# S5 by chunks of four state tiles, with two sums on GpSimd, and routing three rows earlier

## The chip, the cores and the metric

One core of one Trainium2 chip runs the whole kernel as one program. The time is device microseconds of one execution; less is better. TensorE is called PE here, VectorE DVE, ScalarE ACT, GpSimd POOL and SyncE SP.

## What is computed

A decoder trunk of two layers over 256 tokens of width 1024, all in float32. Layer 0 is attention and a gated unit behind one input product; layer 1 is an S5 state-space layer with a sigmoid GLU. Behind each comes a PEER expert layer, and a norm at the end. The change touches S5, its GLU, the norms and the routing of PEER. Cut to these:

```python
def s5_block(h, ...):                       # 64 groups of 16 channels, 64 complex states each
    xr = einsum('bsgc,gpc->bsgp', u, bbr)   # input product, real; xi alike
    # complex diagonal recurrence over the tokens, per state:
    _, _, sr, si = associative_scan(combine, (a_r, a_i, xr, xi), axis=1)
    y = einsum('bsgp,gcp->bsgc', sr, c_re) - einsum('bsgp,gcp->bsgc', si, c_im)
    g = gelu(y + d_skip * h)
    return g * sigmoid(g @ glu_w + glu_b)

def peer(h, wq, subkeys, u_tab, v_tab):
    q = (h @ wq).reshape(t, 8, 2, 128)      # 8 heads, two halves
    sc = einsum('thpc,pkc->thpk', q, subkeys)
    # top 16 of 128 in each half, top 16 of their 256 sums: idx, gate = softmax
    act = gelu(einsum('td,tkd->tk', h, u_tab[idx]))
    return einsum('tk,tkd->td', gate * act, v_tab[idx])
```

## The kernel before, in words

**Rows of experts.** PEER is most of the work. For each of 2 layers, 2 token tiles of 128 tokens and 8 heads there is a group of 16 chosen experts per token: 32 groups, 512 rows. One row is one gather of the u and v rows of 128 experts (one per token), 128 x 2048 floats or 1 MB, issued by POOL (L434) into one of nine ring buffers; a dot product on DVE of the u half with `h` (`dot_product`, L1264); three small instructions on ACT that make gelu times gate and a diagonal matrix of it (`weights`, L620, L623, L626); and two products on PE of the diagonal with the v half (`expert`, L869), which add up in PSUM. POOL issues the gather of row g when the expert products of row g-9 are done. Row r of a phase of 128 rows is called row r below.

**Everything else hangs between the rows.** `between()` writes out by hand which stage runs in which row; every engine walks through the same list and takes the functions that it has. So on each engine the order is fixed: the stages of a row, then on DVE the routing step of that row (`ROUTE`: steps in rows 3, 5, 7, 9 and 11 of each group of 16, for the group that follows), then the row's own dot product. On PE the expert products of row g-1 follow the stages of row g. Layer 1's S5 runs inside phases 1 and 2 (the 128 rows from 128, and from 256), one token tile in each: while DVE and PE do the experts of one token tile of layer 0 they also do S5 of the other.

**S5.** The states are 32 tiles of 128. Before the scan they are turned by the angle of each token, so that the recurrence is a real one, and turned back behind it. The work goes by pairs of state tiles, one pair every five rows from row 9, 16 pairs: PE makes the input product (`s5_in`, L813, 8 matmul records in the trace), DVE turns it (`s5_rot`: L1137 and L1138, products with cosine and sine over 512 elements, then the two sums L1140 and L1141 over 256), two rows later DVE scans (`s5_scan`: L1150, four scans of 128 elements, L1153 and L1154 turn back, L1157 keeps the last state in the first token tile, and every second pair L1104 makes the angles' fraction), and PE makes the output product (`s5_out`, L832, 16 records, into PSUM with tokens as partitions). Two buffers hold the products of the turn. ACT makes the cosine and sine tables for a chunk of four state tiles.

**Behind S5** come `s5_sum` (L1166, L1171: the skip term), `s5_gelu` on ACT, `gate_T` and `gT_copy` (transposes), two GLU products with bias and tanh (`glu_mm` in `stream` L676, `glu_bias` L1182, `glu_sum`), the next norm, and from row 107 four queries, one every five rows (`query`: q_mm in three pieces through L676, transposes, scores). The weights of these products are 2 MB blocks that SP loads into two buffers, each when the product two blocks earlier is done. SP also loads eleven times a vector broadcast to 128 partitions (`load_vec`), two buffers.

**Norms.** `norm_h` (L909) writes x times rstd times gain to `h` for every norm, and PE transposes it.

## Time and profile before

| | |
|---|---|
| median of 3 runs | 1623.54 us (1619.47 to 1626.23) |
| profiled execution | 1625.63 us |
| its span, first to last instruction | 1623.9 us |
| mean granted clock of PE | 0.941 of full |
| read from HBM | 605.19 MB |
| moved by gathers | 536.90 MB |

The profiled execution is 1.7 us longer than its span, which lies outside the instructions. Busy time says how long an engine had work, the lists of waits say what an idle engine waited for, and the stretches say where the DMA queues ran below their best rate.

### The profile page before, as it was taken

Reading aid. Unit: us, or ns where it says so; the run is one execution under the profiler, and the core shown is the slowest. Engines: PE = TensorE matmul, PEld = TensorE weight load, DVE = VectorE, ACT = ScalarE, POOL = GpSimd, SP = SyncE. Lnnn points to the kernel's source line nnn. Section 1 sums busy time; section 2 is a strip of 40 time slices with the busy share of each in tenths; the row PEclk is TensorE's granted clock in tenths of the full one; section 3 lists DMA queues with packets and bytes.
Section 4 is the critical chain, followed back from the end, with each engine's and each line's share of the span. In section 5 each row is a group of like instructions: output and inputs, shape, how many; then the busy total and the mean of one; then the engine's idle time right before and its main releaser. Section 6 shows DMA issues by size and latency. Waiting matters only on the chain. (4 is left out here: it accounts for less than half of the span.)

```text
span 1623.9 us, 15247 instructions
## 1 busy us (share of the span) xinstructions
PE 1372.6 (85%) x3816; PEld 629.7 (39%) x3816; DVE 1140.5 (70%) x2821; ACT 760.9 (47%) x2074; POOL 597.2 (37%) x517
## 2 busy tenths in 40 slices
PE   7999889887697888898999788887898988887776
PEld 3544334433342444454444344444434432222222
DVE  2347865666666898998654898988865486666664
ACT  2325542454344656655443655656433354444443
POOL 0025333343243443334332443433334254444441
PEclk9999899999799898789999998999799999999999
DMA  9569999999799998799999999989899899999996
GB/s 358 185 245 408 409 390 414 383 375 417 302 416 417 418 361 327 313 386 376 405 414 379 416 391 356 342 323 382 326 394 413 315 414 421 422 421 422 422 422 256
DMA packets 106406, 607.22 MB, mean 374 GB/s; under 512 B 9296, under 2 KB 9424, under 8 KB 40784
## 3 DMA queue, kind: packets, MB, share of 16 engines
q0 software_dynamic: 73728, 536.90, 81.9%
q1 hardware_dynamic: 32592, 69.37, 11.5%
q8 instruction: 30, 0.49, 0.1%
q14 instruction: 56, 0.46, 0.1%
HBM read 605.19 MB, written 1.05 MB: 373 GB/s over the span
## 5 line engine op out<-in xcount | busy, mean ns | idle before, releaser
L869 PE MATMUL ps<-rings,dgs 128*128 128x512 f32 x1824 | 902.3, 635 | 179.1 <-ACT dgs L626 178.6
L434 POOL DMA_INDIRECT rings<-in_uv_tab_dram,idx x456 | 530.9, 1164 | 854.0 <-PE ps L869 671.7
L1264 DVE CUSTOM_DVE_ANT_0 rings<-rings,h 128x1024 f32<-128x1024 f32 x456 | 547.5, 1223 | 127.0 <-DMA rings<-in_uv_tab_dram,idx 112.3
L869 PEld LDWEIGHTS ps<-rings,dgs 128*128 128x128 f32 x1824 | 346.7, 200 | 667.2 <-issue 345.7
L620 ACT ACTIVATE gel<-dots 128x1 f32<-128x1 f32 x512 | 103.1, 201 | 548.2 <-DVE dots L1264 537.6
L626 ACT ACTIVATE dgs<-cst,wgt 128x128 f32<-128x128 f32 x512 | 206.2, 403 | 37.0 <-issue 2.5
L676 PE MATMUL ps<-wst,hT 128*128 128x512 f32 x384 | 180.0, 607 | 10.4 <-DMA wst<-in_wq_dram 8.1
L623 ACT ACTIVATE wgt<-gel,share 128x1 f32<-128x1 f32 x512 | 151.5, 296 | 37.5 <-issue 2.8
L869 PE MATMUL ps<-dgs 128*128 128x512 f32 x224 | 113.5, 631 | 17.6 <-ACT dgs L626 17.6
L676 PEld LDWEIGHTS ps<-wst,hT 128*128 128x128 f32 x384 | 73.9, 195 | 103.3 <-issue 101.7
L434 POOL DMA_INDIRECT dgs<-in_uv_tab_dram,idx x56 | 65.0, 1161 | 104.2 <-PE ps L869 95.0
L1041 DVE COPY mem<-ps 128x512 f32<-128x512 f32 x16 | 11.1, 692 | 119.2 <-PE ps L668 119.2
L1264 DVE CUSTOM_DVE_ANT_0 dgs<-dgs,h 128x1024 f32<-128x1024 f32 x56 | 68.5, 1223 | 17.2 <-DMA dgs<-in_uv_tab_dram,idx 15.0
L869 PEld LDWEIGHTS ps<-dgs 128*128 128x128 f32 x224 | 42.4, 199 | 78.8 <-issue 41.3
L620 ACT ACT_TABLE_LOAD x56 | 71.8, 1283 | 1.8
L832 PE MATMUL ps<-mem 128*128 128x32 f32 x512 | 67.7, 288 | 0.0
L832 PEld LDWEIGHTS ps<-mem 128*128 128x128 f32 x512 | 65.1, 205 | 6.6 <-issue 3.5
L676 PE MATMUL ps<-rings,hT 128*128 128x512 f32 x128 | 58.8, 611 | 2.0 <-DVE scr L936 1.2
L510 ACT ACTIVATE mem<-ps 128x512 f32<-128x512 f32 x16 | 9.6, 597 | 88.2 <-PE ps L676 88.2
L1264 DVE DVE_READ_ACCUMULATOR2_ANT dots<- 128x1 f32 x512 | 42.3, 83 | 0.0
L607 ACT ACT_TABLE_LOAD x32 | 41.1, 1283 | 0.8
L1137 DVE TENSOR_TENSOR mem<-ps,mem 128x512 f32<-128x512 f32 x32 | 22.0, 689 | 21.2 <-issue 10.7
(177 smaller groups left out, 973.5 us busy)
## 6 DMA issues: line engine op xcount, KB each, us to landing
wst<-in_wq_dram SPq DMA_DIRECT2D x15, 2048.0 KB
wst<-in_w_out_dram SPq DMA_DIRECT2D x4, 2048.0 KB
wst<-in_glu_w_dram SPq DMA_DIRECT2D x4, 2048.0 KB
rings<-in_uv_tab_dram,idx POOLq DMA_INDIRECT x456
rings<-in_w_in_dram SPq DMA_DIRECT2D x3, 2048.0 KB, 16.6
vec<-in_vecs_dram SPq DMA_DIRECT2D x11, 512.0 KB
rings<-in_w_in_dram SPq DMA_DIRECT2D x2, 1024.0 KB, 8.7
dgs<-in_w_in_dram SPq DMA_DIRECT2D x1, 2048.0 KB, 19.4
```

The lines of the kernel that those rows point to most:

```text
L434: nc.gpsimd.indirect_dma_start(out=ring[g % RING], out_offset=None, in_=uv_tab, in_offset=bass.IndirectOffsetOnAxis(ap=idx[n % 4][:, s:s + ...
L510: A.activation(qs, ps[:, 2, :], ACT.Copy).then_inc(qs_act, 1)
L607: A.activation(gexp[n % 2][:, :], cs[n % 2][:, :], ACT.Exp, bias=ncs[n % 2][:, :], accum_out=gsum[n % 2][:, :]).then_inc(exp_ok, 1)
L620: A.activation(gel[i][:, every], dots[i][:, every], ACT.Gelu_apprx_tanh)
L623: A.activation(wgt[i][:, c], gel[i][:, c], ACT.Copy, scale=share[i][:, c])
L626: A.activation(diag[:, (g + k) % DIAGS, :], ident, ACT.Copy, scale=wgt[i][:, c]).then_inc(diag_ok, 1)
L676: ins = PE.matmul(ps[:, bank, :], lhs[:, k, :], rhs[:, k, :], start=(k == 0), stop=(k == KC - 1))
L832: ins = PE.matmul(o, d, m[:, j, v, :], start=(q == 0), stop=(q == 3))
L869: ins = PE.matmul(ps[:, 4 + 2 * t + b, :], diag[:, g % DIAGS, :], ring[g % RING][:, D + b * BANK:D + (b + 1) * BANK], start=(g % (PH * TOP ...
L1041: V.tensor_copy(qT, four(3)).then_inc(qt_dve, 1)
L1137: V.tensor_tensor(by_cos, x4, cos, ALU.mult)
L1264: V.tensor_tensor_reduce(out=u, in0=u, in1=h[:, t, :], scale=1.0, scalar=0.0, op0=ALU.mult, op1=ALU.add, accum_out=dots[n % 2][:, s:s + 1] ...
```

## The change

What it does, by parts:

- **S5 by chunks.** A chunk of four state tiles every ten rows takes the place of two pairs. Turn and back-turn are two instructions each over 1024 elements, the scans two over 512: the four tiles' scans of 128 tokens lie end to end, and the decay tensor (`s5_decay`, written by ACT) is zero at each first token, which starts a new scan. The state that is carried to the second token tile is added to its first element. There is one buffer for each product of the turn in place of two.
- **The two sums on POOL** (`s5_add`): 512 elements each, all operands in SBUF. POOL does the stages of row r ahead of the gather of row r+7. DVE's scan waits for them (`add_ok`).
- **The input product ahead.** `s5_in` of a chunk stands seven rows ahead of its slot, into the other half of each PSUM bank.
- **Output product turned round.** `s5_out` has the 32-column C matrices as weights and the states as moving data, so that y comes out with channels as partitions; the skip term is one more matmul with a diagonal of `d_skip`. So gelu writes straight into `hT`; `s5_sum`, `gT_copy` and the copy of the transpose fall away, and `gate_T` only makes the g that `glu_sum` multiplies by. The GLU bias is a one-row matmul.
- **Norms.** The mixing norms no longer write `h`: PE multiplies x by a diagonal of rstd, the gain goes in at the copy; the first two norms transpose x itself, and rstd is put in behind the input product. Vectors are loaded three times in place of eleven, plus one small table and two rows of 4 KB.
- **Slots.** Routing steps stand in rows 0, 2, 4, 6 and 8 of a group. GLU begins at row 89, the norm at row 97, and the queries at row 103, one every six rows. `q_copy` and `q_score` come one row later in a query and `q_keep` two. `route_index` does both halves in one instruction each.

The core of the diff, first the order of the work:

```diff
 GROUPS = 2 * T * PH
 RING = 9
+AHEAD = 7
 PACE = 1
...
-ROUTE = {3: "route_keys", 5: "route_pairs", 7: "route_best", 9: "route_index", 11: "route_gate"}
-EXP_AT = 9
+ROUTE = {0: "route_keys", 2: "route_pairs", 4: "route_best", 6: "route_index", 8: "route_gate"}
+EXP_AT = 6
...
-PRELUDE = [("norm_sq", 0), ("norm_ms", 0), ("norm_sd", 0), ("norm_h", 0), ("norm_T", 0), ("hT_copy", 0),
+PRELUDE = [("norm_T", 0), ("hT_copy", 0), ("norm_sq", 0), ("norm_ms", 0), ("norm_sd", 0), ("norm_r", 0),
...
-        at(n, slot + 5, ("q_copy", phase, b))
-        at(n, slot + 6, ("q_score", phase, b))
-        at(n, slot + 7, ("q_keep", phase, b))
+        at(n, slot + 6, ("q_copy", phase, b))
+        at(n, slot + 7, ("q_score", phase, b))
+        at(n, slot + 9, ("q_keep", phase, b))
...
+    def mix_norm(n, slot, m):
+        for i, name in enumerate(("norm_sq", "norm_ms", "norm_sd", "norm_r", "norm_d", "norm_T", "hT_copy")):
+            at(n, slot + i, (name, m))
...
-        norm(g, 3, 4 + 2 * t)
-        for pair in range(S5_TILES // 2):
-            slot = 9 + 5 * pair
-            at(g, slot, ("s5_mm", t, pair))
-            at(g, slot + 1, ("s5_rot", t, pair))
-            at(g, slot + 2, ("s5_turns", t, pair))
-            at(g, slot + 3, ("s5_scan", t, pair))
-            at(g, slot + 4, ("s5_tables", t, pair))
-        at(g, 89, ("s5_last", t))
-        at(g, 90, ("s5_sum", t))
-        at(g, 91, ("s5_gelu", t))
-        at(g, 92, ("gate_T", t))
-        at(g, 93, ("gT_copy", t))
+        mix_norm(g, 3, 4 + 2 * t)
+        at(g, 3, ("s5_turns", t, 0))
+        at(g, 4, ("s5_frac", t, 0))
+        at(g, 6, ("s5_tables", t, 0))
+        for c in range(KC):
+            slot = 11 + 10 * c
+            at(g, slot - 1 if c == 0 else slot - 7, ("s5_in", t, c))
+            at(g, slot, ("s5_decay", t, c))
+            at(g, slot + 1, ("s5_rot", t, c))
+            at(g, slot + 2, ("s5_add", t, c))
+            at(g, slot + 3, ("s5_scan", t, c))
+            at(g, slot + 4, ("s5_cmat", t, c))
+            at(g, slot + 5, ("s5_back", t, c))
+            if c + 1 < KC:
+                at(g, slot + 3, ("s5_turns", t, c + 1))
+                at(g, slot + 4, ("s5_frac", t, c + 1))
+                at(g, slot + 6, ("s5_tables", t, c + 1))
+            at(g, slot + 6, ("s5_out", t, c))
+            if c % 4 == 3:
+                at(g, slot + 8, ("s5_gelu", t, c // 4))
...
-            at(g, 94 + 2 * b, ("glu_mm", t, b, 0, 4))
-            at(g, 95 + 2 * b, ("glu_mm", t, b, 4, 8))
-            at(g, 96 + 2 * b, ("glu_bias", t, b))
-            at(g, 97 + 2 * b, ("glu_sig", t, b))
-            at(g, 98 + 2 * b, ("glu_sum", t, b))
-        norm(g, 101, 5 + 2 * t)
+            at(g, 89 + 2 * b, ("glu_mm", t, b, 0, 4))
+            at(g, 90 + 2 * b, ("glu_mm", t, b, 4, 8), ("gate_T", t, b))
+            at(g, 93 + 2 * b, ("glu_sig", t, b))
+            at(g, 94 + 2 * b, ("glu_sum", t, b))
+        norm(g, 97, 5 + 2 * t)
         for b in range(4):
-            query(g, 107 + 5 * b, 2 + t, b)
+            query(g, 103 + 6 * b, 2 + t, b)
...
         turns, whole = part(4864, 512, a=4), part(5376, 512, a=4)
-        prod = [[part(5888 + 1024 * i + 512 * v, 512, "p (i r s) -> p i r s", i=2, r=2) for v in range(2)]
-                for i in range(2)]
-        zst = part(7936, 512, "p (i r s) -> p i r s", i=2, r=2)
...
+        by_cos, by_sin = (part(5888 + 1024 * v, 1024, "p (r j s) -> p r j s", r=2, j=4) for v in range(2))
+        decay = part(7936, 512, a=4)
```

and then the functions, those that are new or wholly rewritten as they stand after:

```python
            def s5_add(t, c):

                pool.wait_ge(w_ok, KC * t + c + 1)
                G = nc.gpsimd
                G.tensor_tensor(by_cos[:, 0, :, :], by_cos[:, 0, :, :], by_sin[:, 1, :, :], ALU.add)
                G.tensor_tensor(by_cos[:, 1, :, :], by_cos[:, 1, :, :], by_sin[:, 0, :, :], ALU.subtract).then_inc(add_ok, 1)
...
            for g in range(GROUPS * TOPK):
                n, s = g // TOPK, g % TOPK
                if g >= RING:
                    run(WORK[(g - AHEAD) // TOPK].get((g - AHEAD) % TOPK, []))
...
            def norm_d(m):
                act.wait_ge(r_ok, MIX_NORMS.index(m) + 1)
                if m == 6:
                    act.wait_ge(yc_done, KC)
                A.activation(one_diag[:, :], ident, ACT.Copy, scale=rstd[:, NORM_T[m]:NORM_T[m] + 1]).then_inc(rd_ok, 1)
...
            def s5_decay(t, c):

                ci = KC * t + c
                if ci == 0:
                    act.wait_ge(cz_zero, 3)
                else:
                    act.wait_ge(sn_done, ci)
                A.activation(decay[:, :, 1:P], dec[:, 4 * c:4 * c + 4].unsqueeze(2).to_broadcast([P, 4, P - 1]),
                             ACT.Copy).then_inc(dt5_ok, 1)
...
            def s5_gelu(t, half):

                act.wait_ge(yc_done, KC * t + 4 * (half + 1))
                A.activation(hTs[t][:, 4 * half:4 * half + 4, :], four(4 + 2 * t + half),
                             ACT.Gelu_apprx_tanh).then_inc(g_ok, 1)
...
            def s5_in(t, c):

                ci = KC * t + c
                if c == 0:
                    wait_hT(4 + 2 * t)
                    pe.wait_ge(bT_act, 4)
                    banks_2_3()
                if ci >= 2:
                    pe.wait_ge(w_ok, ci - 1)
                for r in range(2):
                    for j in range(4):
                        rows = slice(32 * j, 32 * j + 32)
                        at = 2 * P * (c % 2) + P * r
                        ins = PE.matmul(ps[:, j, at:at + P], bT[rows, 2 * c + r, :], hTs[t][rows, c, :],
                                        start=True, stop=True)
                ins.then_inc(xs_done, 1)

...
            def s5_out(t, c):

                ci = KC * t + c
                pe.wait_ge(d_ok, 2 * (ci + 1))
                pe.wait_ge(cz_ok, 6 * (ci + 1))
                pe.wait_ge(dd_ok, ci + 1)
                bank, cols_ = 4 + 2 * t + c // 4, slice(P * (c % 4), P * (c % 4) + P)
                m = cmat[ci % 2]
                PE.matmul(ps[:, bank, cols_], one_diag[:, :], hTs[t][:, c, :], start=True, stop=False)
                terms = ((by_cos, 0, 0), (by_sin, 1, 1), (by_sin, 0, 2), (by_cos, 1, 2))
                for q, (z_, r, v) in enumerate(terms):
                    for j in range(4):
                        ins = PE.matmul(ps[32 * j:32 * j + 32, bank, cols_], m[:, j, v, :], z_[:, r, j, :],
                                        start=False, stop=(q == 3))
                ins.then_inc(yc_done, 1)
...
            def norm_r(m):

                t = NORM_T[m]
                dve.wait_ge(sd_done, m + 1)
                V.reciprocal(rstd[:, t:t + 1], sd[:, t:t + 1]).then_inc(r_ok, 1)
                dve.drain()
                if m < 2:
                    dve.wait_ge(ld_cst, 16)
                    for w in (cos_t, sin_t, nsin_t):
                        V.tensor_scalar(w[:, t, :], w[:, t, :], rstd[:, t:t + 1], None, ALU.mult)
                    dve.drain()
...
            def s5_rot(t, c):

                ci = KC * t + c
...
                x4 = ps[:, 0:4, 2 * P * (c % 2):2 * P * (c % 2 + 1)].rearrange("p j (r s) -> p r j s", r=2)
                V.tensor_tensor(by_cos, x4, cos, ALU.mult)
...
                V.tensor_tensor(by_sin, x4, sin, ALU.mult).then_inc(w_ok, 1)
...
            def s5_scan(t, c):

                dve.wait_ge(add_ok, KC * t + c + 1)
                if t == 1:

                    V.tensor_tensor(by_cos[:, :, :, 0], by_cos[:, :, :, 0], z_last[:, :, 4 * c:4 * c + 4], ALU.add)
                    dve.drain()
                dve.wait_ge(dt5_ok, KC * t + c + 1)
                for r in range(2):
                    w = by_cos[:, r, :, :].rearrange("p j s -> p (j s)")
                    ins = V.tensor_tensor_scan(w, decay.rearrange("p j s -> p (j s)"), w, 0.0, ALU.mult, ALU.add)
                ins.then_inc(sn_done, 1)
                dve.drain()
                if t == 0:
                    V.tensor_copy(z_last[:, :, 4 * c:4 * c + 4], by_cos[:, :, :, P - 1])

...
            def s5_back(t, c):

                cos, sin = s5_tabs(KC * t + c)
                V.tensor_tensor(by_sin, by_cos, sin, ALU.mult).then_inc(d_ok, 1)
                dve.drain()
                V.tensor_tensor(by_cos, by_cos, cos, ALU.mult).then_inc(d_ok, 1)
```

## Rows read from the trace of the kernel before

**Rows 1.** The page of the profile, part 1: busy time of each engine.

```profile
PE 1372.6 (85%) x3816; PEld 629.7 (39%) x3816; DVE 1140.5 (70%) x2821; ACT 760.9 (47%) x2074; POOL 597.2 (37%) x517
```

**Rows 2.** Busy time in stretches of 40 us: PE, PEld, DVE, ACT, POOL, clock, DMA share, GB/s.

```profile
600.00:640.00 40.00, 32.89 (x119) 16.85 (x118) 37.91 (x99) 21.19 (x58) 14.45 (x12) 0.87 0.89 341
1160.00:1200.00 40.00, 39.40 (x96) 19.55 (x97) 20.46 (x40) 14.21 (x39) 10.82 (x9) 0.85 0.94 355
1240.00:1280.00 40.00, 34.75 (x96) 16.56 (x95) 20.52 (x58) 13.46 (x37) 10.65 (x10) 0.96 0.93 359
1400.00:1440.00 40.00, 31.81 (x63) 11.31 (x63) 27.52 (x71) 16.88 (x51) 17.01 (x17) 0.96 1.01 422
```

**Rows 3.** Line L1137, first token tile, then second: ns min/median/max, first and last start.

```profile
L1137 DVE TENSOR_TENSOR mem<-ps,mem x16: 684/689/692, 529.9 to 748.4; 128x512 f32<-128x512 f32 x16
...
L1137 DVE TENSOR_TENSOR mem<-ps,mem x16: 685/688/692, 924.7 to 1146.1; 128x512 f32<-128x512 f32 x16
```

**Rows 4.** Timeline of DVE, one pair of state tiles: start us, us, instruction.

```profile
541.20 0.69 DVE L1137 TENSOR_TENSOR mem<-ps,mem 128x512 f32<-128x512 f32 x1
...
543.46 1.22 DVE L1264 CUSTOM_DVE_ANT_0 dgs<-dgs,h 128x1024 f32<-128x1024 f32 x1
...
545.75 1.36 DVE L1150 TENSOR_TENSOR_SCAN mem<-s5s,mem 128x128 f32<-128x128 f32 x4
...
548.76 0.69 DVE L1104 SCALAR_TENSOR_TENSOR mem<-mem 128x512 f32<-128x512 f32 x1
549.37 1.22 DVE L1264 CUSTOM_DVE_ANT_0 rings<-rings,h 128x1024 f32<-128x1024 f32 x1
```

**Rows 5.** Groups by line and shape: busy us, mean ns, idle before.

```profile
L832 PE MATMUL ps<-mem 128*128 128x32 f32 x512 | 67.7, 288 | 0.0
...
L1150 DVE TENSOR_TENSOR_SCAN mem<-s5s,z_init,mem 128x128 f32<-128x128 f32 x64 | 25.8, 465 | 0.0
...
L1150 DVE TENSOR_TENSOR_SCAN mem<-s5s,mem 128x128 f32<-128x128 f32 x64 | 21.9, 404 | 0.0
...
L1140 DVE TENSOR_TENSOR mem<-mem 128x256 f32<-128x256 f32 x32 | 13.6, 425 | 2.4
...
L1166 DVE TENSOR_TENSOR h<-h,vec 128x1024 f32<-128x1024 f32 x2 | 2.4, 1220 | 0.0
```

**Rows 6.** Timeline of POOL and DVE: gathers beside dot products, and the one elementwise instruction.

```profile
39.04 1.09 POOL L423 TENSOR_SCALAR_AFFINE_SELECT sgw<-sgw 128x1024 f32<-128x1024 f32 x1 [38.52 <-DMA sgb<-in_sgu_bT_dram]
...
783.24 0.94 POOL L434 DMA_INDIRECT rings<-in_uv_tab_dram,idx  x1 [3.79 <-PE ps L869]
...
788.25 1.22 DVE L1264 CUSTOM_DVE_ANT_0 rings<-rings,h 128x1024 f32<-128x1024 f32 x1
...
788.39 1.90 POOL L434 DMA_INDIRECT rings<-in_uv_tab_dram,idx  x1 [4.21 <-PE ps L869]
```

**Rows 7.** Timeline of PE: S5 in, S5 out, one expert row, half a weight product.

```profile
615.75 0.79 PE L813 MATMUL ps<-hT,mem 32*128 32x128 f32 x8
616.48 1.97 PE L832 MATMUL ps<-mem 128*128 128x32 f32 x16
...
781.08 1.88 PE L869 MATMUL ps<-rings,dgs 128*128 128x512 f32 x4
...
782.80 3.60 PE L676 MATMUL ps<-wst,hT 128*128 128x512 f32 x8
```

**Rows 8.** Waits: engine, line waited for, us in total, times, longest.

```profile
POOL rings L434 <- DVE idx L1248: 149.3, 19, 62.0
...
DVE mem L1182 <- PE ps L676: 26.6, 4, 8.0
...
PE ps L676 <- DMA wst<-in_wq_dram: 8.1, 2, 5.2
```

**Rows 9.** DMA issues, and the first work of PE.

```profile
vec<-in_vecs_dram SPq DMA_DIRECT2D x11, 512.0 KB
...
8.61 1.94 PE L668 MATMUL ps<-cst,h 128*128 128x128 f32 x8 [8.61 <-DVE h L909]
```

More of the change, by code:

```diff
@@ L457, in norm_sd @@
                 A.activation(sd[:, t:t + 1], ms[:, t:t + 1], ACT.Sqrt).then_inc(sd_done, 1)
+            def norm_d(m):
[3 more added lines that the diff above has]
+                A.activation(one_diag[:, :], ident, ACT.Copy, scale=rstd[:, NORM_T[m]:NORM_T[m] + 1]).then_inc(rd_ok, 1)
             def hT_copy(m):
                 act.wait_ge(nT_done, 2 * m + 1)
-                A.activation(hTs[NORM_T[m]][:, 0:4, :], four(0), ACT.Copy).then_inc(hT_act, 1)
+                hT = hTs[NORM_T[m]]
+                if m in MIX_NORMS:
+                    act.wait_ge(ld_col, 16)
+                    g = mix_gain[MIX_NORMS.index(m)]
+                    for k in range(4):
+                        ins = A.activation(hT[:, k, :], ps[:, 0, k * P:(k + 1) * P], ACT.Copy, scale=g[:, k:k + 1])
+                    ins.then_inc(hT_act, 1)
+                else:
+                    A.activation(hT[:, 0:4, :], four(0), ACT.Copy).then_inc(hT_act, 1)
             def z_out(zi):
@@ L691, in norm_T @@
                     pe.wait_ge(p_done, 2)
-                pe.wait_ge(h_done, m + 1)
-                for b in range(2):
-                    turn(b, h[:, NORM_T[m], b * BANK:(b + 1) * BANK], nT_done)
+                if m < 2:
+                    pe.wait_ge(ld_x[t], 16)
+                elif m in MIX_NORMS:
+                    pe.wait_ge(rd_ok, MIX_NORMS.index(m) - 1)
+                else:
+                    pe.wait_ge(h_done, FFN_NORMS.index(m) + 1)
+                for b in range(2):
+                    if m < 2:
+                        turn(b, x[:, t, b * BANK:(b + 1) * BANK], nT_done)
+                    elif m in MIX_NORMS:
+                        for a in range(4):
+                            ins = PE.matmul(ps[:, b, a * P:(a + 1) * P], x[:, t, b * BANK + a * P:b * BANK + (a + 1) * P],
+                                            one_diag[:, :], start=True, stop=True)
+                        ins.then_inc(nT_done, 1)
+                    else:
+                        turn(b, h[:, t, b * BANK:(b + 1) * BANK], nT_done)
             def z(zi, k0, k1):
@@ L1162, in s5_sum @@
-            def s5_sum(t):
-                v = D_VEC[t]
-                dve.wait_ge(ld_vec[v % 2], 16 * (v // 2 + 1))
-                V.tensor_tensor(h[:, t, :], h[:, t, :], vec[:, v % 2, :], ALU.mult).then_inc(dh_done, 1)
-                dve.drain()
-                dve.wait_ge(yc_done, 16 * (t + 1))
-                for b in range(2):
-                    hs = h[:, t, b * BANK:(b + 1) * BANK]
-                    V.tensor_tensor(hs, hs, ps[:, 4 + 2 * t + b, :], ALU.add).then_inc(ye_ok, 1)
```

374 lines of the change are left out of this document (169 added, 205 removed).

## The prediction, made before any run of the changed kernel

> **What bounds the kernel now.** The busy shares come first [rows 1]: PE 85%, DVE 70%, neither full. So the answer lies by stage. In the stretches [rows 2] there is one where nothing but experts runs (1400 to 1440): the DMA queues move 422 GB/s at a share of 1.01, DVE has 27.5 of 40 us busy. A gather of 1.049 MB then takes 1.049/422 = 2.485 us, and that is the least a row can take. In the S5 stretch (600 to 640) it is the other way: 341 GB/s, and DVE has 37.9 of 40 us. The starts of the first product of the turn say it exactly [rows 3]: 16 pairs, so 15 steps of five rows, from 529.9 to 748.4, which is 29.13 us for ten rows, and 29.52 in the second token tile, against 24.85 by DMA. DVE bounds S5; DMA bounds nearly all else. Outside S5, stretches fall short of 422 GB/s by 6.4 us of DMA time in GLU (1160 to 1200, (422 - 355)/422 x 40) and 6.0 in the queries (1240) [rows 2].
>
> **DVE in S5, before.** From the timeline [rows 4]: turn with sums 543.46 - 541.20 = 2.26 us; two dot products to 545.75, 1.145 each; scans, back-turn and copy to 548.76, 3.01; fraction 0.61. A chunk of four tiles is two pairs and one fraction: 4.52 + 6.02 + 0.61 = 11.15 us.
>
> **DVE in S5, after.** An instruction of 1024 elements lasts 1.22 us [rows 5] and the next one starts 1.145 later, as the dot products show. The turn is two of them and a drain: 2.37. A scan of 128 elements lasts 404 ns, about what a product of 256 does (425) [rows 5], so I take a scan of 512 as a product of 1024: 1.15, two and a drain 2.37. What was left in the 3.01 beside four scans (1.36) and two products (1.22) is 0.43 for copy and drains: 0.4 stays. Back-turn with an inner drain 2.45, fraction 0.61. Sum 8.20, so 2.95 less a chunk. A chunk's ten rows also save 0.25 for `route_index` (three pairs of instructions become three single ones, each 0.14 shorter, 10/16 of the time). In the second token tile the old scans take 465 ns, not 404: another 0.49 saved, while the addition of the carried state costs some 0.25. Ten rows: 29.13 - 3.20 = 25.93, and 29.52 - 3.44 = 26.08, if the sums cost DVE nothing.
>
> **The two sums on POOL.** The trace shows no sum of two SBUF operands on POOL. The nearest row is its one elementwise instruction, 1.09 us for 1024 elements of one input [rows 6]; the sums read 2 x 512, so I take 1.09 each, 0.55 from below, 2.2 from above. The Trainium skill, GPSIMD Engine Reference, section Performance versus the Vector engine, has 4497 ns for a sum over 2048 elements, which makes an estimate of 1.12 us for 512 and would leave the total as it is; no run here shows it.
> POOL and DVE also stand in each other's way. The gather's instruction at 783.24 lasts 0.94 us with DVE idle; the one at 788.39 lasts 1.90, and a dot product ran from 788.25 to 789.47 [rows 6]. 1.90 less the 1.08 to its end is 0.82: POOL stood still until the dot product was over. What the trace can't show is the reverse, DVE waiting for POOL, since a gather's instruction reads only a column of indices. I take it to hold as well, since a path that lets one in at a time stops either: behind the turn come dot product, sum, dot product, sum, and only then the scan. DVE loses 2 x 1.09 + 0.17 for handing over, 2.35, in five of eight chunks; in three (turns in rows 32, 52 and 82, with a routing step made mostly of one-input searches ahead of the dot product) about 1.2. Mean 1.9. Bounds: 0.2 (no exclusion: 2.5 for the sums against 2.29 for the two dot products) and 4.6 (sums of 2.2). So ten rows take 27.8 and 28.0; saved 1.3 and 1.5 us a chunk, times eight: **23 us**. POOL's wait for the turn (`w_ok`) holds up one gather in ten by some 2 us, with six or seven more under way: nothing, unless DMA bounds the stretch, and it doesn't.
> The Trainium skill, SBUF — State Buffer, section Who interferes with whom, says that a DVE instruction with two SBUF inputs and a POOL instruction that reads SBUF exclude each other for the whole instruction, whichever came first. The trace agrees on POOL's side, by that 1.90; by this rule alone the change would get the 23 us, without it 50.
>
> **PE, ACT in S5.** PE: an expert row is 782.80 - 781.08 = 1.72 us, S5 in 0.73 and out 1.80 to 1.97 a pair [rows 7]; ten rows 17.2 + 1.6 + 3.9 = 22.7 at full clock, at the 0.87 granted there [rows 2] 26.1. After: 34 records of 128 columns in place of 32, each 0.1 as those of S5 in (0.79/8): 3.4 to 4.2. Nothing, covered by DVE's 27.8, but only just: if DVE got down to 26, PE would decide. ACT gets two instructions more per chunk, of 128 and 508 elements, about 1 us together if an element costs it what it costs DVE, at 21 of 40 us busy: nothing; if it were late, the scan would wait.
>
> **GLU.** DVE stood 26.6 us over four waits for the GLU products [rows 8], dot products queued behind it. Now tanh reads PSUM on ACT and `glu_sum` comes three to four rows behind the product; `s5_sum`, the bias and a copy leave DVE (1.22 and five of 0.69, 4.7 us a tile). Bounds 0 and 12.8, twice the 6.4 us by which DMA fell short: I take **5**.
> **Queries.** PE waited 8.1 us for weights whose buffer comes free only two queries earlier [rows 8]; six rows for a query in place of five give twelve rows in place of ten. Bounds 0 and 8.1, taken **6**. `q_keep` of the first query is in row 112, where `route_keys` now is too: DVE waits some us, idle anyway there.
> **Vectors.** Eight loads of 512 KB fewer [rows 9], 1.24 us each where DMA bounds; some fall in S5 where it doesn't: 0 to 9.9, taken **5**.
> **Prelude and routing.** PE starts at 8.61, waiting for the norm [rows 9]; it now needs only x, but then the first weights. 0 to 4, taken **1**. Gathers waited 149.3 us for indices, 62.0 of it at the start [rows 8]; three rows earlier ends most of the other 87, but where DMA is full they cost nothing: 0 to 5, taken **1**.
>
> **Sum.** 23 + 5 + 6 + 5 + 1 + 1 = 41. The profiled execution took 1625.6 us (span 1623.9 and 1.7 around it), so 1584.6; the median of the three runs is 2.1 lower, so **1583 us**.
>
> **Rivals.**
> *No exclusion on DVE's side (0.20).* Ten rows 26.1 to 26.3; S5 gives 3.0 and 3.2 a chunk, 50 us in all, 68 with the rest: 1556. For it: no DVE instruction in the trace is longer beside POOL. Against it: POOL's own standing still.
> *The sums are dearer than 1.09 (0.13).* At 1.6 each DVE loses 1.0 more a chunk, 16 us: 1599; at 2.2 it loses 35 us: 1618.
> *Nothing measurable (0.05).* DVE is relieved, but another engine takes over at the same pace, ACT's tables or PE at 0.87: only the 18 us outside S5 could come, and half of those: within 8 us of before, 1616 to 1631.
> *Slower, by PE (0.04).* The new output product writes 32-row strips in one bank and swaps weights at every record. If these aren't pipelined, each takes the 0.288 us that a record lasts [rows 5] in place of 0.12: 34 x 0.288 = 9.8, 5.9 more a chunk, PE 28.6 in ten rows and 32.9 at clock 0.87, against 29.3 now: 3.6 x 16 = 58 us more, less the 18 from outside S5: 1623.5 + 40 = 1664. It decides from about 0.2 us a record. Against it: S5 in is of the same size and runs at 0.1.
>
> **Numbers.** Exclusion on both sides, as summed, has 0.58. Half a per cent, 8 us, is about what a measurement of this kernel can tell from no change. Faster by more: 0.58 + 0.20 + 0.12 = 0.90; within: 0.06; slower: 0.04. The range runs from 1550 (no exclusion, and a little more from GLU and vectors) to 1606 (sums of 1.6, half of the other gains).
>
> **What would show it.** Ten rows of S5, by the starts of the turn: 27.8 (forecast), 26.1 (no exclusion), over 29 (wrong). The dot product after the turn at 2.3 us in place of 1.22, or its start put off, beside a sum of POOL of 1.1 to 2.3 us. Scans near 1.2 us. S5 out under 4.2 us a chunk on PE. DVE's wait for GLU gone from the list, PE's wait for weights near 0, gathers waiting for indices under 80 us. DMA moved 4 MB less. The forecast is wrong if the scan doesn't wait for the sums, or if PE or ACT is what DVE waits for in S5.

## The result, and the profile after

The changed kernel takes 1637.1 us (median; 1633.7 to 1640.5) against 1623.54 (1619.47 to 1626.23): 1.0085 times as long, interval 1.0061 to 1.011. It was forecast at 1583, at most 1606. It is slower by 14 us, and on none of the mechanisms that the prediction gave for slower.

The page of the profile, part 1, shows the relief that was wanted [rows 1]: DVE does 56 us less, PE 37 us less, and still the span is 12.5 us longer.

```profile
PE 1335.2 (82%) x3872; PEld 584.9 (36%) x3872; DVE 1084.1 (66%) x2493; ACT 768.2 (47%) x2120; POOL 617.5 (38%) x549
```

Three of the stretches of 40 us of [rows 2] (same columns):

```profile
600.00:640.00 40.00, 29.89 (x115) 12.52 (x113) 29.56 (x60) 19.65 (x52) 19.20 (x17) 0.83 0.86 329
1160.00:1200.00 40.00, 32.24 (x103) 13.88 (x102) 25.45 (x50) 14.87 (x46) 12.53 (x11) 0.91 0.92 353
1400.00:1440.00 40.00, 32.63 (x66) 11.51 (x64) 26.42 (x68) 16.13 (x51) 15.90 (x16) 0.97 1.01 421
```

In S5 (600 to 640) DVE was busy 37.9 us of 40; now it is 29.6, and the queues still bring no more (329 GB/s against 341). So DVE has room and stands still. The first instruction of the turn (L1200 now), first and last start in each token tile, as in [rows 3]:

```profile
L1200 DVE TENSOR_TENSOR mem<-ps,mem x8: 1219/1220/1225, 533.9 to 743.0; 128x1024 f32<-128x1024 f32 x8
...
L1200 DVE TENSOR_TENSOR mem<-ps,mem x8: 1218/1218/1221, 938.3 to 1151.8; 128x1024 f32<-128x1024 f32 x8
```

Seven steps of ten rows in 209.1 and 213.5 us: 29.87 and 30.50 for ten rows, where 29.13 and 29.52 stood and 27.8 and 28.0 were forecast. What DVE waits for is in the list of waits (engine, line waited for, us in total, times, longest):

```profile
POOL rings L467 <- DVE idx L1291: 60.6, 1, 60.6
...
DVE mem L1209 <- POOL mem L448: 36.6, 8, 7.7
...
DVE mem L1214 <- POOL mem L448: 33.0, 8, 7.2
...
DVE mem L1231 <- ACT mem L641: 30.3, 4, 8.2
DVE tiny L1298 <- ACT gexp L648: 28.2, 6, 9.9
...
PE ps L717 <- DMA wst<-in_wq_dram: 9.4, 4, 3.3
```

L1209 and L1214 are the scan stage (with and without a carried state), L448 is the second sum on POOL. DVE waits for it in all 16 chunks, 69.6 us together, 4.35 a chunk. In the groups by line and shape (busy us, mean ns, idle before) no instruction is so dear that it could explain the loss: 1.22 us for a scan of 512 (1.15 from start to start was forecast), 1.31 and 1.33 for the sums (1.09 forecast), and 17.3 us of records for the output product, 1.08 a chunk (3.4 to 4.2 forecast):

```profile
L1214 DVE TENSOR_TENSOR_SCAN mem<-mem 128x512 f32<-128x512 f32 x32 | 37.8, 1223 | 33.9 <-POOL mem L448 33.0 <-issue 0.4
L448 POOL TENSOR_TENSOR mem<-mem 128x512 f32<-128x512 f32 x16 | 21.3, 1332 | 0.0
L447 POOL TENSOR_TENSOR mem<-mem 128x512 f32<-128x512 f32 x16 | 21.0, 1312 | 0.3
...
L888 PE MATMUL ps<-mem 128*32 128x128 f32 x512 | 17.3, 276 | 0.0
```

Why the sums come late shows in the timeline of one chunk (all engines, start us, us; DVE's turn ended at 590.7):

```profile
589.50 12.26 PE L921 MATMUL ps<-rings,dgs 128*128 128x512 f32 x24 [3.51 <-ACT dgs L667]
...
593.78 1.22 DVE L1307 CUSTOM_DVE_ANT_0 dgs<-dgs,h 128x1024 f32<-128x1024 f32 x1
...
595.17 0.94 POOL L467 DMA_INDIRECT rings<-in_uv_tab_dram,idx  x1 [0.50 <-PE ps L921]
...
596.89 0.94 POOL L467 DMA_INDIRECT rings<-in_uv_tab_dram,idx  x1 [0.78 <-PE ps L921]
...
598.61 0.94 POOL L467 DMA_INDIRECT rings<-in_uv_tab_dram,idx  x1 [0.78 <-PE ps L921]
599.57 1.27 POOL L447 TENSOR_TENSOR mem<-mem 128x512 f32<-128x512 f32 x1
600.79 1.27 POOL L448 TENSOR_TENSOR mem<-mem 128x512 f32<-128x512 f32 x1
...
602.09 2.34 DVE L1214 TENSOR_TENSOR_SCAN mem<-mem 128x512 f32<-128x512 f32 x2 [7.08 <-POOL mem L448]
602.35 1.98 PE L921 MATMUL ps<-dgs 128*128 128x512 f32 x4
...
608.57 3.78 PE L921 MATMUL ps<-rings,dgs 128*128 128x512 f32 x4 [4.24 <-ACT dgs L667]
```

POOL works in program order. The sums of row r stand at its loop index r + `AHEAD` = r + 7, so behind the gather of row r + 6, and that gather needs the buffer of expert r + 6 - 9 = r - 3. The three gathers ahead of the sums are each released by PE, one expert row (1.72 us) apart; the sums start only at 599.57, nine us after their operands were ready at 590.7. PE's clock adds to it: PE had stood for 3.51 us before 589.50, its granted clock in the stretch 590 to 594 was 0.57, and its records there start 0.86 us apart, where they start 0.43 apart from 594 on, at a clock of 1.00. Meanwhile DVE has done the dot product that ends at 595.0 and stands for 7.08 us, and PE, which works off seven expert rows meanwhile (589.5 to 604.3), has then no dot product left to work on and stands for 4.24 us. The scan is in row r + 1, so in every chunk DVE can't be more than four rows ahead of PE, whatever the ring of nine would hold; the two stand in turn.

Three theories followed from this reading. **Lead**: the cost is that wait. **Price**: the cost is what the sums do to DVE by exclusion (POOL and DVE can't run such instructions at once), dearer than forecast. **Bursts**: the cost is outside the sums, in the moved routing and the longer stages, several of which meet in one row.

### The profile page after: what moved, and what is told of

Its sections match the earlier page's. It is cut to its first block, busy times and chain, and to the rows that moved or that the text cites. A ratio compares the mean times of both kernels' runs of the same rounds, so it can differ in the third digit from the quotient of the medians.

```text
span 1636.4 us, 15020 instructions
## 1 busy us (share of the span) xinstructions
PE 1335.2 (82%) x3872; PEld 584.9 (36%) x3872; DVE 1084.1 (66%) x2493; ACT 768.2 (47%) x2120; POOL 617.5 (38%) x549
## 2 busy tenths in 40 slices
DMA packets 105402, 603.12 MB, mean 369 GB/s; under 512 B 9314, under 2 KB 9442, under 8 KB 39780
## 3 DMA queue, kind: packets, MB, share of 16 engines
HBM read 601.08 MB, written 1.05 MB: 368 GB/s over the span
## 4 chain that ended last, share of the span: by engine, by line
PE 39%; DMA 20%; DVE 18%; ACT 10%; POOL 4%; DVEq 3%; issue 3%; ACTq 2%; SPq 0%; POOLq 0%
PE ps L921 23%; DMA rings<-in_uv_tab_dram,idx 13%; PE ps L717 11%; DVE rings L1307 6%; DMA wst<-in_wq_dram 4%; ACT L661 2%; DMA mem<-in_s_b_dram 2%; PE ps L910 2%; ACT dgs L667 1%; ACTq L603 1%; ACT wgt L664 1%; POOL rings L467 1%; POOL mem L448 1%; POOL mem L447 1%; DVE mem L1225 1%
## 5 line engine op out<-in xcount | busy, mean ns | idle before, releaser
L467 POOL DMA_INDIRECT rings<-in_uv_tab_dram,idx x456 | 515.2, 1130 | 855.0 <-PE ps L921 761.6
L467 POOL DMA_INDIRECT dgs<-in_uv_tab_dram,idx x56 | 59.1, 1055 | 96.4 <-PE ps L921 91.0
L717 PEld LDWEIGHTS ps<-wst,hT 128*128 128x128 f32 x320 | 60.8, 193 | 86.1 <-issue 84.6
L1214 DVE TENSOR_TENSOR_SCAN mem<-mem 128x512 f32<-128x512 f32 x32 | 37.8, 1223 | 33.9 <-POOL mem L448 33.0
L717 PEld LDWEIGHTS ps<-rings,hT 128*128 128x128 f32 x128 | 24.5, 198 | 32.8 <-issue 30.4
```

The source lines that it names most:

```text
L467: nc.gpsimd.indirect_dma_start(out=ring[g % RING], out_offset=None, in_=uv_tab, in_offset=bass.IndirectOffsetOnAxis(ap=idx[n % 4][:, s:s + ...
L717: ins = PE.matmul(ps[:, bank, :], lhs[:, k, :], rhs[:, k, :], start=(k == 0), stop=(k == KC - 1))
L1214: ins = V.tensor_tensor_scan(w, decay.rearrange("p j s -> p (j s)"), w, 0.0, ALU.mult, ALU.add)
```

## The experiments

| run | kernel | median us | ratio to before (95%) | ten rows of S5, us |
|---|---|---|---|---|
| | changed | 1637.1 | 1.0085 (1.0061 to 1.011) | 29.87, 30.50 |
| 1 | sums on DVE | 1587.73 | 0.9769 (0.9726 to 0.9812) | 26.89, 27.10 |
| 2 | scan two rows later | 1620.41 | 0.9979 (0.996 to 0.9999) | 29.1, 29.5 |
| 3 | `AHEAD` 5 | 1611.42 | 0.9922 (0.9891 to 0.9952) | 28.27, 28.53 |
| 4 | `AHEAD` 8 | 1664.37 | 1.0245 (1.0208 to 1.0283) | 31.5, 31.8 |
| 5 | sums on DVE, spare sums on POOL | 1616.03 | 0.9973 (0.9953 to 0.9992) | 28.7, 28.7 |
| 6 | sums on DVE, spare memsets on POOL | 1591.43 | 0.9822 (0.9793 to 0.9851) | 26.9, 27.1 |
| 7 | sums on DVE, routing in rows 3 to 11 | 1565.70 | 0.9664 (0.9638 to 0.969) | 26.4, 26.6 |
| 9 | changed, routing in rows 3 to 11 | 1624.25 | 1.001 (0.9996 to 1.0023) | 29.3, 30.1 |
| 10 | sums on DVE, gate step in row 11 | 1590.86 | 0.9799 (0.9759 to 0.9839) | 26.6, 26.8 |
| 12 | sums on DVE, old routing in first groups | 1580.25 | 0.9729 (0.9693 to 0.9765) | 26.9, 27.1 |
| 13 | sums on DVE, routing in rows 1 to 9 | 1566.37 | 0.9656 (0.9612 to 0.9701) | 26.5, 26.7 |
| 14 | sums on DVE, routing in rows 4 to 12 | 1566.86 | 0.9659 (0.9621 to 0.9697) | 26.7, 26.9 |
| 8 | sums on DVE, S5's B loaded earlier | 1571.51 | 0.9704 (0.9675 to 0.9734) | 26.9, 27.1 |
| 11 | 8, and routing in rows 3 to 11 | 1554.73 | 0.9584 (0.956 to 0.9608) | 26.5, 26.6 |

Each ratio is to the kernel before as measured beside that row, and its median there was between 1619.2 and 1623.5 us. Runs 1 to 4 were measured beside each other, and so were 5 to 8. A difference between other rows is known to some 5 us only: where the text below takes it from the medians, the ratios give 17 us in place of 22 for the routing (runs 1 and 7), 11 in place of 16 for the load (1 and 8), and 33 in place of 28 for the spare sums (1 and 5).

**1. The sums back on DVE.** POOL has no stage any more; the rest of the change stands.

```diff
-                V.tensor_tensor(by_sin, x4, sin, ALU.mult).then_inc(w_ok, 1)
+                V.tensor_tensor(by_sin, x4, sin, ALU.mult)
+                dve.drain()
+                V.tensor_tensor(by_cos[:, 0, :, :], by_cos[:, 0, :, :], by_sin[:, 1, :, :], ALU.add)
+                V.tensor_tensor(by_cos[:, 1, :, :], by_cos[:, 1, :, :], by_sin[:, 0, :, :], ALU.subtract).then_inc(w_ok, 1)
...
-                dve.wait_ge(add_ok, KC * t + c + 1)
```

> The changed kernel with the two sums back on DVE, right behind the turn. Three theories. Lead: the sums stand in POOL's order behind the gather of row r+6, which waits for the expert products of row r-3, so at each chunk DVE can be no more than four rows ahead of PE, and waits. Price: the sums themselves cost, 1.3 us each in place of 0.6, and they shut DVE's dot products out while they run. Bursts: chunks of 8 us of DVE work leave ACT and PE idle, wherever the sums are. Lead and price expect the same here: ten rows of S5 at 27.4 us (25.9 and the sums at 1.4), against 29.9 and 30.5 in the changed kernel, so 1637 - 44 = 1593 us. Bursts expects ten rows at 29 or more and 1625 us or more.

Measured 1587.73: 49 us faster than the changed kernel, and 36 faster than before. So all that was lost, and more, hangs on the place of two sums, and bursts, which expected 1625 or more here, is out as the main cause. The stretch 600 to 640 is now

```profile
600.00:640.00 40.00, 29.91 (x137) 12.93 (x137) 36.19 (x79) 28.46 (x73) 16.31 (x13) 0.93 0.97 392
```

392 GB/s, the clock at 0.93. This does not yet tell lead from price.

**2. The scan two rows later**, with back-turn and output product, the sums on POOL.

```diff
-            at(g, slot + 3, ("s5_scan", t, c))
+            at(g, slot + 5, ("s5_scan", t, c))
...
-            at(g, slot + 5, ("s5_back", t, c))
+            at(g, slot + 7, ("s5_back", t, c))
...
-            at(g, slot + 6, ("s5_out", t, c))
+            at(g, slot + 8, ("s5_out", t, c))
```

> The changed kernel with the scan, the back-turn and the output product two rows later in each chunk; the sums stay on POOL where they are. Lead: DVE may now be six rows ahead of PE when it needs the sums; its waits for POOL fall from 69.6 us to under 20, ten rows take about 27, and the time is about 1597. Price: the dot products that now stand beside the sums are longer or late by 2.4 us a chunk, so waits turn into longer dot products: over 1620. Bursts: no change, within 5 us of 1637.

DVE's wait for POOL is gone from the list altogether, and 17 us with it, fewer than the lead theory alone asks for (it expected 1597). Two things took its place. There is one buffer for the turned input, so DVE's turn now waits for the output product of the chunk before; and dot products got longer:

```profile
DVE mem L1200 <- PE ps L888: 23.0, 11, 4.7
```

```profile
1049.07 3.75 DVE L1307 CUSTOM_DVE_ANT_0 rings<-rings,h 128x1024 f32<-128x1024 f32 x1
...
1082.15 4.02 DVE L1307 CUSTOM_DVE_ANT_0 rings<-rings,h 128x1024 f32<-128x1024 f32 x1
```

(the second fence is DVE's timeline of the same kernel). A dot product that takes 1.22 us alone takes 4.02 where it meets both sums. Nine of the 512 take over 1.35 us, where the changed kernel has one (2.28), and DVE's busy time on the page of the profile is 1108.0 us against 1084.1.

**3, 4. `AHEAD` 5 and 8** in place of 7, in the changed kernel: the sums stand two gathers further forward, or one further back.

> The changed kernel with AHEAD = 5: POOL does the sums of row r ahead of the gather of row r+5, not r+7, so only the gathers up to r+4 and with them the expert products up to r-5 stand before them. Lead: DVE's waits for POOL fall from 69.6 us to under 20, as with the later scan, less what gathers lose that now wait for the turn; 1600. Price and bursts: no change, within 5 us of 1637.

> The changed kernel with AHEAD = 8: the sums of row r behind the gather of row r+7, so behind the expert products of row r-2. Lead: DVE may be three rows ahead of PE only; its waits for POOL grow from 69.6 us to 100 or more and the time by 20 to 30, to 1660. Price and bursts: no change, within 5 us of 1637.

The wait for POOL's sums, of 69.6 us at 7, is (first fence `AHEAD` 5, second 8)

```profile
DVE mem L1209 <- POOL mem L448: 13.6, 4, 5.2
DVE mem L1214 <- POOL mem L448: 12.1, 4, 3.7
```

```profile
DVE mem L1214 <- POOL mem L448: 50.5, 8, 10.5
DVE mem L1209 <- POOL mem L448: 47.1, 8, 8.9
```

25.7, 69.6 and 97.6 us of waiting go with 1611.4, 1637.1 and 1664.4 us of time. From 7 to 8 nothing changes but the place of the sums in POOL's queue; 28 us more waiting cost 27 us. With 5, six dot products of 2.27 to 2.65 us appear, and DVE is busy for 1100.2 us: once the wait is short, exclusion shows. Time moves with the place of the sums in both directions, where price and bursts expected no change. So lead is shown as a cause, and price remains beside it.

**5, 6. The price by itself.** Kernel 1 with two more sums a chunk on POOL, of a constant table into a spare buffer that nobody reads or waits for; and the same with four memsets in their place, which read nothing.

```diff
+                pool.wait_ge(add_ok, 2 * (KC * t + c))
+                for i in range(2):
+                    G.tensor_tensor(spare[:, i, :], cst[:, C_CNT:C_CNT + BANK], cst[:, C_CNT:C_CNT + BANK], ALU.add).then_inc(add_ok, 1)
```

(Shown are the new lines of the first; in the second, the two sums are four memsets of the same buffer.)

> The kernel with the sums on DVE (1587.7 us), and POOL does at each chunk, where its sums stood, two sums over 512 elements of a constant table into a spare buffer for which nobody waits. No wait of DVE hangs on POOL, so what is left is what a POOL instruction that reads SBUF does to DVE, and the one gather in ten behind it. Exclusion on both sides: dot products of 2.3 us beside the sums, sums of up to 2.3 us, DVE loses 1.5 to 2.4 us a chunk, 16 chunks, 1612 to 1625. No exclusion on DVE's side: within 4 us of 1588.

> The same, but POOL fills the spare buffer (four fills of 512 elements) and reads nothing. If what shuts the dot products out is POOL's reading beside DVE's second input: no dot product over 1.35 us beside the fills, and within 4 us of 1588. If any POOL instruction shuts them out, as the sums did: over 1600. If the loss is only POOL's time and late gathers, both kernels lose alike.

The spare sums cost 28.3 us over kernel 1, and the memsets 3.7, which the intervals do not tell from nothing; the two, measured beside each other, are 24.6 us apart. The memsets stand in the same place, wait for the turn in the same way and take 2.05 us a chunk, as the two sums below do, so POOL's waiting and the late gathers are not what costs. DVE's busy time grows as the time does, by 27.9 us with the sums and 1.7 with the memsets (first line the sums on DVE, 1102.5, then with spare sums, 1130.4; memsets 1104.2):

```profile
PE 1324.5 (83%) x3872; PEld 579.3 (36%) x3872; DVE 1102.5 (69%) x2525; ACT 768.2 (48%) x2120; POOL 588.6 (37%) x517
PE 1330.6 (82%) x3872; PEld 580.8 (36%) x3872; DVE 1130.4 (70%) x2525; ACT 768.5 (48%) x2120; POOL 633.7 (39%) x549
```

The timeline of the kernel with spare sums shows it once in full:

```profile
627.76 3.72 DVE L1313 CUSTOM_DVE_ANT_0 rings<-rings,h 128x1024 f32<-128x1024 f32 x1
628.34 2.05 POOL L452 TENSOR_TENSOR spare<-cst 128x512 f32<-128x512 f32 x2
```

The record of the dot product begins 0.58 us ahead of the first sum, while a gather's instruction was still running, and ends 1.09 us behind the second. It took 3.72 us: 1.22 and 2.50. With memsets no dot product exceeds 1.30 us. Small DVE instructions do not always escape the memsets: this copy, 0.17 us as a rule, ends only when the first two memsets are through, and in two places a conversion of 0.15 us lasts 1.28 and 1.34.

```profile
728.66 1.69 DVE L1226 COPY z_last<-mem 128x8 f32<-128x8 f32 x1
729.32 2.05 POOL L454 MEMSET spare<- 128x512 f32 x4
```

28.3 us over 16 chunks are 1.77 a chunk, where the forecast took 1.9. A spare sum lasts 1.03 to 1.21 us when nothing holds it, the sums of the changed kernel 1.27, so for those the price may be a little higher. The Trainium skill, SBUF — State Buffer, section Who interferes with whom, has the exclusion between a DVE instruction with two SBUF inputs and POOL's reads that these two runs show, on either side.

**7. The routing back in its old rows**, first with the sums on DVE, then (9) in the changed kernel.

```diff
-ROUTE = {0: "route_keys", 2: "route_pairs", 4: "route_best", 6: "route_index", 8: "route_gate"}
-EXP_AT = 6
+ROUTE = {3: "route_keys", 5: "route_pairs", 7: "route_best", 9: "route_index", 11: "route_gate"}
+EXP_AT = 9
```

> The kernel with the sums on DVE (1587.7 us), and the routing steps back in rows 3, 5, 7, 9 and 11 of a group. If the earlier slots are worth what the prediction took for them, 1 us (0 to 5): 1588 to 1593. If S5's slots and the routing's collide less in the old ones: under 1585. POOL's waits for indices come back to some 80 us beside the first one.

> The changed kernel (1637 us) with nothing but the routing steps put back in rows 3, 5, 7, 9 and 11; the sums stay on POOL. With the sums on DVE that was worth 22 us. If the two parts of the change cost independently of each other: 1612 to 1620. If the wait for POOL at each chunk hides the routing's cost, since PE is given time there: 1630 or more.

Moving the routing ahead costs 22 us with the sums on DVE (17 by the ratios), and 13 in the changed kernel, though POOL then waits less for indices (127.0 us at the old rows, 60.6 at the new). Why was asked in four runs.

**10. The gate step alone in its old row (11).** It waits for ACT's exponential, 26 us in all with the new rows.

> The kernel with the sums on DVE and the routing in its new rows (1587.7 us), but with the last step, the gate's reciprocal, in row 11 and not in row 8. There DVE waits 26.1 us over six times for ACT's exponential of row 6, which stands behind ACT's other work of that row. If this in-order wait is what the earlier routing costs: 1566 to 1575, and the waits for the exponential are gone. If it is rather that routing steps and S5 steps now fall into the same rows, or into the first rows of a phase with the norm: within 5 us of 1588.

1590.86, against 1587.73: no gain. DVE's wait for the exponential is not the cause.

**12. The old rows in the first group of each weight phase only.**

> Sums on DVE, the old routing rows only in the first group of each weight phase (n = 8, 16, 24), the new rows in the other groups. Theory first rows: the earlier routing costs where it stands in the same rows as the first tables of S5, the row sums and the normalised row of a phase, so in the first group: 1566 to 1573 us, near the 1565.7 of the run with the old rows everywhere, and the gathers at 144, 272 and 400 come about 5 to 8 us earlier than with the new rows, beginning after those points. Theory spread: it costs in every group, so that three of thirteen groups give back at most 5 us: 1583 to 1592 us.

1580.25 lies between the two ranges, so neither theory holds: 7.5 of the 22 us. The cost is neither in those groups alone nor absent there.

**13, 14. Rows 1, 3, 5, 7, 9 and rows 4, 6, 8, 10, 12.** The heavy stages of a chunk stand in rows 12 (turn), 14 (scan) and 16 (back-turn) plus ten a chunk, all even.

> Sums on DVE, routing in rows 1, 3, 5, 7, 9 and the exponential in row 7: two rows earlier than in the kernel before, one row later than in the changed one. Theory parity: turn, scan and back-turn of a chunk stand in rows 12, 14 and 16 plus ten a chunk, which are all even; at even rows a routing step comes between such a stage and the dot product of its row, so that one dot product is put off by both (5.3 us between two dot products in the timeline of the run with the sums on DVE, back-turn and route_best); at odd rows it stands between two light ones. Then this run takes 1563 to 1572 us, as the one with rows 3 to 11 (1565.7). Theory earliness (the earlier, the dearer, whatever the reason): two thirds of the cost stays, 1577 to 1584 us.

> Sums on DVE, routing in rows 4, 6, 8, 10, 12 and the exponential in row 10: one row later than in the kernel before, but even. Theory parity: it costs as the changed kernel's rows do, 1580 to 1592 us. Theory earliness: nothing is earlier than before, 1560 to 1568 us.

Both take what rows 3 to 11 take (1566.4, 1566.9, 1565.7). Each theory is right on one run and wrong on the other. The starts of the dot products in the four traces say more; this table is worked out from them, over phases 1 and 2 together (us for the first 16 rows of the two phases, for rows 16 to 80, which hold six of the eight chunks, and for rows 80 to 128, the end of S5, GLU and queries):

```
routing rows        rows 0 to 16   rows 16 to 80   rows 80 to 128   sum
0, 2, 4, 6, 8       112.4          341.5           313.4            767.2
1, 3, 5, 7, 9        96.6          336.4           309.1            742.2
3, 5, 7, 9, 11      101.6          338.6           301.7            741.9
4, 6, 8, 10, 12     106.4          341.8           297.8            746.0
```

These are single executions. Two other runs with rows 0 to 8 (6 and 8) give 111.5 to 112.0, 341.3 to 341.6 and 309.1 to 316.8, and one with rows 3 to 11 (11) gives 102.9, 338.8 and 302.5, so the last column but one is the least sure. In rows 16 to 80 odd routing rows are faster than even ones, as parity says, but by 3 to 5 us only (run 10, with nothing but the gate step in an odd row, has 336.8 there, and still gains nothing in all). In rows 80 to 128 each later placement takes less, as earliness says, by 4 to 16 us. In the first 16 rows all three gain on the rows of the changed kernel, by 6 to 16 us, the odd ones most. What parity does shows in DVE's timeline with the sums on DVE and even rows, with rows of routing between these lines:

```profile
597.43 1.22 DVE L1223 TENSOR_TENSOR mem<-mem 128x1024 f32<-128x1024 f32 x1
598.75 1.23 DVE L1225 TENSOR_TENSOR mem<-mem 128x1024 f32<-128x1024 f32 x1
599.89 0.42 DVE L1266 MAX8 cs<-cand 128x8 f32<-128x256 f32 x1
...
602.14 0.42 DVE L1276 FIND_INDEX8 pos_i<-cs,cand 128x8 uint32<-128x256 f32 x1
602.69 1.23 DVE L1307 CUSTOM_DVE_ANT_0 rings<-rings,h 128x1024 f32<-128x1024 f32 x1
603.84 1.22 DVE L1307 CUSTOM_DVE_ANT_0 rings<-rings,h 128x1024 f32<-128x1024 f32 x1
```

and with rows 1 to 9:

```profile
596.63 1.22 DVE L1223 TENSOR_TENSOR mem<-mem 128x1024 f32<-128x1024 f32 x1
597.94 1.22 DVE L1225 TENSOR_TENSOR mem<-mem 128x1024 f32<-128x1024 f32 x1
599.08 1.22 DVE L1307 CUSTOM_DVE_ANT_0 rings<-rings,h 128x1024 f32<-128x1024 f32 x1
600.23 0.42 DVE L1266 MAX8 cs<-cand 128x8 f32<-128x256 f32 x1
...
602.47 0.42 DVE L1276 FIND_INDEX8 pos_i<-cs,cand 128x8 uint32<-128x256 f32 x1
603.02 1.23 DVE L1307 CUSTOM_DVE_ANT_0 rings<-rings,h 128x1024 f32<-128x1024 f32 x1
```

DVE's work is the same, but in the first a dot product starts 5.26 us behind the start of the back-turn (597.43 to 602.69) and then two come at once; in the second they are 3.94 apart. PE and the buffers that it frees follow the dot products, and a row's pace by DMA is 2.49. That this is what the 3 to 5 us are is read from the timeline and was not tried by itself. For rows 80 to 128, DVE's wait for the scores in `route_keys` (13.1 us in four waits in row 0, 1.9 in one in row 1) may explain some. The rest, and the cost in the first 16 rows, stay open: what makes up most of the routing's price is not shown.

**8, 11. S5's B loaded ahead of weight blocks 9 and 10.** The chain that ended last (start us, us, what) has, in the changed kernel,

```profile
377.82 31.21 DMA mem<-in_s_b_dram
```

This load of 512 KB stands behind weight blocks of 2 MB, 9 and 10 the last of them. Only its place in SP's order is changed, so these two now stand behind it and behind its wait:

```diff
-            load_w(7, 8, 9, 10)
+            load_w(7, 8)
             sp.wait_ge(mix_done, T)
             sp.dma_start(b_raw, s5_b).then_inc(ld_b, 16)
+            load_w(9, 10)
```

> The kernel with the sums on DVE (1587.7 us), and the S5 input matrix loaded ahead of the weight blocks 9 and 10 and not behind them. It landed at about 409 us while DVE waited 14.1 us for it and PE 22 us behind DVE, and the DMA queues ran dry: 268 GB/s from 400 to 440, 14.6 us of DMA time lost. If that stall is on the path, the wait of DVE is 0 and the time falls by 9 to 13 us, to 1576; if the gain is given back to the weights' own loads, under 4 us.

> Sums on DVE, routing steps in rows 3 to 11, and the S5 input matrix loaded ahead of the weight blocks. The single parts gave 1565.7 and, for the load, 16 us. If they add: 1548 to 1554.

1571.51, 16 us less than kernel 1 (11 by the ratios); the gather of row 112 starts 15 us earlier, and the wait (15.2 us in kernel 1) has gone. With the old routing rows as well it is 1554.73, 4.2% faster than the kernel before, the fastest of all. That is just above the 1548 to 1554 expected: next to run 7, where the wait for the load was 11.4 us, the earlier load gives 11 us (13 by the ratios) and not 16. Its stretch 600 to 640:

```profile
600.00:640.00 40.00, 31.13 (x125) 13.05 (x123) 38.51 (x77) 25.34 (x77) 20.31 (x16) 0.96 0.98 399
```

DVE is at 38.5 of 40 again, and DMA at 0.98: in this stretch the two bounds have nearly met.

## Why the prediction was wrong

The direction was wrong, and one step did it.

**The step that failed** is "POOL's wait for the turn (`w_ok`) holds up one gather in ten by some 2 us, with six or seven more under way: nothing". It asked what the sums do to the gathers, and never what the gathers do to the sums. The sums stand in program order behind a gather that needs expert r - 3, and DVE's scan, one row on, waits for them. The prediction had `AHEAD = 7` and the ring of nine before it; the subtraction was not made. The wait was not among the rivals either.

**What that wait costs.** Kernel 1 without its two sums would take an estimated 1568.2 us: 1587.7, less 19.5 for the sums (one ends 0.61 us after the one before in the timelines, 2 x 0.61 x 16). DVE would then be busy for 1083.0 us by the page. To this are added DVE's waits for POOL's sums and what DVE is busy above 1083.0, which is what exclusion adds:

```
kernel              waits for POOL   busy above 1083.0   estimate   measured
changed             69.6             1.1                 1638.9     1637.1
AHEAD 5             25.7             17.2                1611.1     1611.4
AHEAD 8             97.6             -0.1                1665.7     1664.4
scan later           0               25.0                1593.2     1620.4
```

The last has besides 23.0 us of waits for the output product, which make it 1616.2. Run 9, worked out from run 7 in the same way, comes to 1546.2 + 61.4 + 15.8 = 1623.4 (measured 1624.25). So in S5 nearly every us that DVE waits is a us of time, and the changed kernel loses 1637.1 - 1568.2 = 68.9 us by the wait for the sums, where the prediction had nothing. Exclusion, for which it had 1.9 us a chunk or 30 in all, costs about 1: DVE stands still while POOL adds. The wait came in its place.

**DVE's own sum was right.** Ten rows were put at 25.93 and 26.08 without the sums; with the sums on DVE (1.22 more: 27.15 and 27.30) they measure 26.89 and 27.10. The scan of 512 was put at 1.15 a start and lasts 1.22.

**Exclusion was right as a fact, and its price was not paid here.** 1.09 a sum was taken, 1.27 to 1.33 measured, so [rows 6]'s one-input instruction of 1024 elements is 0.2 short for a two-input one of 2 x 512. The estimate of 1.12 us from the Trainium skill, GPSIMD Engine Reference, section Performance versus the Vector engine, falls short as well for these, though some spare sums took 1.05. Exclusion was put at 1.9 us a chunk and measures 1.77 where POOL's sums meet a busy DVE (run 5). Exclusion on both sides, the disputed assumption, is shown, and the rival's assumption (0.20) is out. In the changed kernel itself one dot product of 512 was held.

**Routing was priced at 1 us gained and costs 13.** "Where DMA is full they cost nothing: 0 to 5" looked only at POOL's wait for indices, which did fall by 89 us and bought nothing. That a routing step is DVE work (1.7 us for `route_keys`, 2.7 for `route_best`) whose row matters was not looked at. "DVE waits some us, idle anyway there", of `route_keys` beside `q_keep`, is neither borne out nor refuted: its waits for scores are 8.4 us in three, against 8.7 in three before, and more in kernel 1 (13.1 in four). The forecast of 1583, less 30 us for exclusion, plus 68.9 for the wait and 14 for the routing, gives 1636, against 1637.1 measured; that it closes so well is partly chance, since the smaller terms missed both ways.

**The smaller terms.** *GLU* (5): the wait did not go, 30.3 us in four waits against 26.6 [rows 8], now behind tanh on ACT in place of the product. *Queries* (6): the wait for weights is 9.4, not near 0. *Vectors* (5): 603.12 MB moved, 4.1 less, as said; where it shows can't be told. *Prelude* (1): the first gather starts 2.4 us earlier. *S5 out*: PE needs 1.08 us for 32 records in the changed kernel, where 16 took 1.97 [rows 7], so a chunk is about 1.4 us with the skip records (614.87 to 616.26 in the lines at the end) in place of 3.9. It was put at 3.4 to 4.2, and the rival that goes slower by it was far off.

*Not counted*: the first group of a phase. From the gather of row 128 to that of 144, and 256 to 272, the changed kernel takes 56.3 and 57.6 us, where before took 45.3 and 43.4. The first chunk's tables, row sums and norm stand there together; the old routing rows give back 6 and 8 of the 11 and 18 that kernel 1 loses there. What costs the rest wasn't tried.

**The range.** It took in the bounds of each unknown duration, and none of an unknown wait. The 0.04 for slower stood for one mechanism that was priced, not for those that nobody had thought of.

## What to carry to other kernels

When a stage is moved to another engine, find the instruction ahead of it on that engine's queue, follow what releases that one, and subtract in rows: here ring depth and look-ahead leave the sums waiting for an expert three rows back, and their reader one row on. An in-order queue full of gathers is a bad place for work that somebody waits for, even if it is idle 60% of the time. Try the rows of side work one by one: here moving five steps by one row was worth some 20 us, and no simple rule told which way. Put a small load that gates a stage ahead of the large ones that don't.

## What the runs showed of the hardware

- A dot product of DVE with two SBUF inputs is held for the whole of several POOL instructions in a row: 3.72 us beside two sums, 4.02 at most, 1.22 alone. POOL's sums last up to 2.33 us where they wait in their turn. POOL memsets of 512 elements hold no dot product (64 of them of 0.53 us, none over 1.30), but a few small copies and conversions beside them last 1.28 to 1.69 us in place of 0.15 to 0.17.
- After PE had stood for 3.51 us its granted clock was 0.57 from 590 to 594 us in the changed kernel, and records of 512 columns started 0.86 us apart in place of 0.43.
- An output product with weights of 32 columns and a moving operand of 128 runs 32 records in 1.08 us, one each 0.034; 16 records of the turned form (128-column weights, 32 moving) took 1.97, one each 0.12. Whether the fewer weight columns or the strips that the records write side by side do it wasn't tried.

```profile
614.87 0.38 PE L884 MATMUL ps<-hT,one_diag 128*128 128x128 f32 x2
615.18 1.08 PE L888 MATMUL ps<-mem 128*32 128x128 f32 x32
```
